# A two-layer hybrid decoder trunk on one core: five small reorderings on VectorE, ScalarE and TensorE

## The chip, the cores and the metric

The kernel runs on one core of one Trainium2 chip. The metric is the device time of one execution in microseconds (us), as a median over runs. The engines are called as the profile calls them: PE is TensorE (PEld its weight loads), DVE is VectorE, ACT is ScalarE, POOL is GpSimd, and SP issues most of the DMAs.

## The reference

The reference is a trunk of two layers on a sequence of 512 tokens of width 1024. Each layer is this, cut to what matters here:

```
h = rms_norm(x, norm1_g);  proj = h @ w_in
y_a = gelu(a_u) * (tril(w_spatial) @ rms_norm(gelu(a_v)) + b_spatial)      # mixer A: gMLP
y_b = causal attention, 8 heads, on low-rank q and kv, rotary tail          # mixer B
y_c = gated DeltaNet, 8 heads, chunks of 64, on silu(causal_conv(c_qkv))    # mixer C
      (q and k of each head l2-normalised; a triangular solve in each chunk; a scan over 8 chunks)
y_c = rms_norm(y_c) * silu(c_z)
x = x + (sum_i sigmoid(gate_i) * (y_i @ w_branch[i])) @ w_out
x = x + relu(rms_norm(x) @ w_ff1)^2 @ w_ff2
```

All of it is fp32. The kernel gets near-fp32 matmuls by splitting each large operand into a high and a low part of fp32r and adding three passes (high by high, high by low, low by high).

## The kernel before

The whole stream is held transposed, channels on partitions and the 512 tokens along the free side. All weights come as one stream of 288 units of 512 KB. SP issues their DMAs into a ring of two raw slots, POOL splits each into high and low (lines 408 and 413, one operation each over 128x1024), and PE uses them in a fixed order, `UNITS`. Each engine has its own written-out program, and semaphores with running counts tie them together, so an instruction that waits holds everything behind it on its engine.

PE's unit of work is `project(tile)`: 24 matmuls of 128x512 (lines 445 to 447) into one of two alternating PSUM banks. A later tile of the same bank waits for `bank_read`, which DVE or ACT raise when they have taken the last one out. Small matmuls and transposes of the mixers are set between the projections.

In each layer PE projects the decay row, then twelve tiles k0 to k3, q0 to q3, v0 to v3 (i = 0 to 11). For tile i DVE runs `conv(i)` (lines 1559 to 1566) and ACT `take_conv(i)`: Silu, and for the eight tiles of k and q a Square into the buffer `csq`. PE then sums the squares by head in `sum_squares(i)` (line 535, matmuls with two output columns). `csq` has four slots of 2 KB. In layer 0 DVE also works out the angles of the rotary tables in `rotation_angles(0)` and `(1)`, on tiny tiles.

Then comes the triangular solve. DVE runs 31 rank-one steps (lines 1672 and 1675) and large transposes (1691, 1696), and in between takes tiles that PE has ready: `token_rows(tt)` (lines 1642, 1644, which raise `tok_scaled`) and `take_lat(j)`. PE waits for `tok_scaled` before it transposes `krT` (line 819), and for the last of DVE's transposes before `corner_products` (line 652). ACT places the products of the corner with four copies (line 1232), in two pairs. After that a recurrence of nine steps begins, `recur(step)`: PE, ACT's copy of `vnew` (line 1258), PE again (line 710), DVE's `state`. ACT takes the four z tiles with Silu in `take_z(j)`, and loads the table for Sqrt ahead of the corner copies (line 1227).

While the delta branch is merged, DVE masks the spatial weights with the lower triangle (line 1776, 128x1024, raises `wsp_masked`) between two of its steps. Attention follows: 32 blocks of scores, each with ACT's Exp (line 1348), and for each group of eight blocks `take_sums(i)` (line 1326) and `outputs_high(i)` (1330) on ACT, and `normalise(i)` and `outputs_low(i)` (1886, 1891) on DVE. After the last Exp ACT loads the table for Gelu, runs four Gelus over `avT`, then takes the last sums, squares two tiles of `avT`, runs `outputs_high(3)`, and squares the last two. PE, after a projection of gates, sums those squares in `sum_av` (line 958), then waits for `wsp_masked` and transposes the masked weights (line 961).

ACT holds one table of functions at a time. A table load stands in the profile as ACT_TABLE_LOAD, at the line of the function that needs it, or at the line of an explicit `preload_act_table`. Copy and Square need none of their own.

Of the kernel before, what the change touches and what calls it, by code (L numbers as in the profile page):

```python
# [16 lines left out]
P = 128  # L17
DEPTH = 2
SEQ = 512
# [164 lines left out]
def hybrid_trunk(nc, stream, params, x, positions, constants, out):  # L184

    with ExitStack() as ctx:
# [46 lines left out]
        kqT, vT = at(0, "kqT", [P, 2, PAIRS, SEQ]), at(16, "vT", [P, PAIRS, SEQ])  # L233
        convd, csq = at(84, "convd", tile2), at(56, "csq", [P, 4, SEQ])
        gtok, gone = at(68, "gtok", [P, TT, STACK]), at(69, "gone", [P, 2, TT, HEADS])
# [198 lines left out]
        def _(pe):  # L434
            pe.wait_ge(ident_in, 16)
            for layer in range(DEPTH):
# [93 lines left out]
                def sum_squares(i):  # L530

                    pe.wait_ge(csq_ready, layer * per.csq_ready + i + 1)
                    for t in range(TT):
                        at = (i // 4 * TT + t) * HEADS + 2 * (i % 4)
                        last = mm(S(0)[:, at:at + 2], csq[:, i % 4, t * P:(t + 1) * P], c("ind", i % 4, 8)[:, 2 * (i % 4):2 * (i % 4) + 2],  # L535
                                  start=True, stop=True)
                    last.then_inc(csq_summed, 1)
# [254 lines left out]
                for i in range(12):  # L792
                    if i or layer:
                        project((("k", "q", "v")[i // 4], i % 4))
                    for n in {3: (0,), 4: (1,), 5: (2,), 6: (3,), 7: (4, 5), 8: (6, 7)}.get(i, ()):
                        sum_squares(n)
                    if i == 5:
                        turn_decay()
                    if i == 7:
                        cumulate()  # L800
                    if i == 9:
                        turn_rows()
                        pe.wait_ge(consts_done, 1)
                    if i >= 10:
                        for tt in range(2):
                            chunk_terms(2 * (i - 10) + tt)
# [234 lines left out]
        def _(act):  # L1041
# [50 lines left out]
            for layer in range(DEPTH):  # L1092
# [31 lines left out]
                def take_conv(i):  # L1124
# [5 lines left out]
                    if i < 8:  # L1130
                        act.wait_ge(act_tile, layer * per.act_tile + i + 1)
                        if i >= 4:
                            act.wait_ge(csq_summed, layer * per.csq_summed + i - 3)
                        f(csq[:, i % 4], dst, ACT.Square).then_inc(csq_ready, 1)

# [82 lines left out]
                for hf in range(2):  # L1218
# [5 lines left out]
                    if hf == 0:  # L1224
                        take_z(2)
                take_z(3)
                nc.scalar.preload_act_table(ACT.Sqrt)
                for hf in range(2):
                    for ch in range(2):
                        rows = np.s_[64 * ch:64 * ch + 32]  # L1230
                        act.wait_ge(corner_done, layer * per.corner_done + 2 * hf + ch + 1)
                        nc.scalar.copy(gated[rows, 2 * hf:2 * hf + 2, 0, :, 32:64],
                                       S((4 + 2 * hf + ch) % 6)[rows].rearrange("p (t h s) -> p t h s", t=2, h=HEADS)).then_inc(corner_placed, 1)

                def square_o(tt):
# [9 lines left out]
                def copy_output(step):  # L1245
# [6 lines left out]
                    if step and step % 2 == 0:  # L1252
                        square_o(step // 2 - 1)

                for step in range(CHUNKS + 1):
                    rows = np.s_[0:64] if step == 0 else np.s_[64:128] if step == CHUNKS else np.s_[0:128]
# [80 lines left out]
                for n in range(32):  # L1337
# [14 lines left out]
                    if n % 8 == 6 and n > 8:  # L1352
                        outputs_high(n // 8 - 1)
                nc.scalar.preload_act_table(ACT.Gelu)
                for j in range(4):
                    tile = TILE_NO[("av", j)]
                    act.wait_ge(bank_read[tile % 2], layer * per.bank_read + tile // 2 + 1)
                    f(avT[:, j], avT[:, j], ACT.Gelu).then_inc(av_ready, 1)
                take_sums(3)
                act.wait_ge(av_ready, layer * per.av_ready + 4)  # L1360
# [53 lines left out]
        def _(dve):  # L1414
# [83 lines left out]
            nc.vector.tensor_scalar(tri[:], c("incl"), -1.0, None, ALU.is_ge).then_inc(tri_done, 1)  # L1498
            rotation_angles(0)
            for layer in range(DEPTH):  # L1500
# [90 lines left out]
                for i in range(9):  # L1591
# [9 lines left out]
                    if i == 5:  # L1601
# [6 lines left out]
                        ins.then_inc(g_token, 1)  # L1608
                    if i == 5 and layer == 0:
                        rotation_angles(1)  # L1610
                dve.wait_ge(cum_done, layer * per.cum_done + 1)
# [58 lines left out]
                for k in range(31):  # L1670
# [9 lines left out]
                    if k == 11:  # L1680
                        token_rows(2)
                        take_lat(3)
                    if k == 15:
                        token_rows(3)
                    if k == 17:
                        take_lat(4)
# [76 lines left out]
                def latent(d):  # L1763
# [7 lines left out]
                    if 1 <= d < 6:  # L1771
                        dve.wait_ge(lat_hi, layer * per.lat_hi + d)
                        tt_(latLo[:, d - 1], ltmp[:, (d - 1) % 2], latHi[:, d - 1].bitcast(F32), ALU.subtract).then_inc(lat_lo, 1)
                    if d == 6:
                        dve.wait_ge(tables_in, 64)
                        tt_(p("wsp").rearrange("p (g n) -> p g n", g=8), p("wsp").rearrange("p (g n) -> p g n", g=8),
                            c("tril").unsqueeze(1).broadcast_to([P, 8, P]), ALU.mult).then_inc(wsp_masked, 1)

# [128 lines left out]
                normalise(3)  # L1907
                outputs_low(3)
                nc.vector.memset(biasr[:].bitcast(F32), 0.0).then_inc(vector_step, 1)
                dve.wait_ge(vector_step, steps.next())  # L1910
# [180 lines left out]
```

## Time and profile before

| | |
|---|---|
| median of 3 runs | 1855.63 us (1855.09 to 1856.7) |
| the profiled execution, its own time | 1855.63 us |
| its span, first to last instruction | 1853.8 us |
| mean granted PE clock | 0.998 of full |
| PE busy | 1832.8 us, 99% of the span |
| DVE, ACT, POOL busy | 869.0, 467.0, 1032.4 us |
| weights read | 288 units of 512 KB |

The span is the time between the profile's first and last instruction. The profiled execution's own time is 1.8 us more than its span, and it is also the median of the runs shown. Times in rows are counted from the start of the span. Matmuls are pipelined and their ends are modelled, so the distance between two starts tells more of PE than a duration does. Layer 0 runs to about 925 us and layer 1 repeats it 915.5 us later.

### The profile page before, as it was taken

Reading aid. Unit: us, or ns where it says so; the run is one execution under the profiler, and the core shown is the slowest. Engines: PE = TensorE matmul, PEld = TensorE weight load, DVE = VectorE, ACT = ScalarE, POOL = GpSimd, SP = SyncE. Lnnn points to the kernel's source line nnn. Section 1 sums busy time; section 2 is a strip of 40 time slices with the busy share of each in tenths; the row PEclk is TensorE's granted clock in tenths of the full one; section 3 lists DMA queues with packets and bytes.
Section 4 is the critical chain, followed back from the end, with each engine's and each line's share of the span. In section 5 each row is a group of like instructions: output and inputs, shape, how many; then the busy total and the mean of one; then the engine's idle time right before and its main releaser. Section 6 shows DMA issues by size and latency. Waiting matters only on the chain.

```text
span 1853.8 us, 26960 instructions
## 1 busy us (share of the span) xinstructions
PE 1832.8 (99%) x10428; PEld 1491.7 (80%) x10428; DVE 869.0 (47%) x1283; ACT 467.0 (25%) x872; POOL 1032.4 (56%) x580
## 2 busy tenths in 40 slices
PE   8999999999999999999999999999999999999998
PEld 7887788778888888888888777886788888888887
DVE  8587546543444322323265965465444442414141
ACT  6433315550113000000144242165411230001010
POOL 6534267225666666666653524661456666666662
PEclk9999999999999999999999999999999999999999
DMA  6212033122223333333342211221322233323331
GB/s 229 84 58 80 26 101 104 34 91 91 89 93 107 101 93 100 94 99 96 97 137 69 69 59 54 95 91 35 103 91 91 91 95 98 98 96 98 95 101 70
DMA packets 46762, 167.12 MB, mean 90 GB/s; under 512 B 5018, under 2 KB 8346, under 8 KB 46146
## 3 DMA queue, kind: packets, MB, share of 16 engines
q1 hardware_dynamic: 44066, 154.30, 26.7%
q10 hardware_dynamic: 2592, 11.29, 1.6%
q8 instruction: 83, 1.36, 0.3%
q14 instruction: 21, 0.17, 0.0%
HBM read 159.28 MB, written 6.29 MB: 89 GB/s over the span
## 4 chain that ended last, share of the span: by engine, by line
PE 88%; DVE 9%; issue 1%; ACT 1%; DMA 0%; POOL 0%; SPq 0%; ACTq 0%; DVEq 0%; POOLq 0%
PE ps L445 26%; PE ps L447 25%; PE ps L446 25%; PE ps L897 2%; DVE ps L1675 1%; DVE outer L1672 1%; PE ps L920 1%; DVE lanes L1659 1%; PE ps L907 1%; DVE gated L1696 1%; PE ps L535 1%; DVE acc L1446 1%; PE ps L678 1%; PE ps L710 1%; PE ps L688 1%
## 5 line engine op out<-in xcount | busy, mean ns | idle before, releaser
L413 POOL TENSOR_TENSOR wLo<-wraw,wHi 128x1024 fp32r<-128x1024 f32 x288 | 724.7, 2516 | 23.9
L408 POOL TENSOR_SCALAR wHi<-wraw 128x1024 fp32r<-128x1024 f32 x288 | 307.8, 1069 | 769.5 <-PE ps L447 754.0
L445 PE MATMUL ps<-hHi,wHi 128*128 128x512 f32 x1360 | 545.1, 401 | 1.7 <-DVE gated L1696 1.3
L447 PE MATMUL ps<-hHi,wLo 128*128 128x512 f32 x1360 | 530.9, 390 | 0.0
L446 PE MATMUL ps<-hLo,wHi 128*128 128x512 f32 x1360 | 530.3, 390 | 0.0
L445 PEld LDWEIGHTS ps<-hHi,wHi 128*128 128x128 f32 x1360 | 256.0, 188 | 66.1 <-issue 11.1
L447 PEld LDWEIGHTS ps<-hHi,wLo 128*128 128x128 f32 x1360 | 255.6, 188 | 54.4
L446 PEld LDWEIGHTS ps<-hLo,wHi 128*128 128x128 f32 x1360 | 256.2, 188 | 49.7 <-issue 1.2
L445 PE MATMUL ps<-fHi,wHi 128*128 128x512 f32 x640 | 249.3, 389 | 0.0
L447 PE MATMUL ps<-fHi,wLo 128*128 128x512 f32 x640 | 249.0, 389 | 0.0
L446 PE MATMUL ps<-fLo,wHi 128*128 128x512 f32 x640 | 249.0, 389 | 0.0
L1396 ACT ACTIVATE fHi<-relu 128x512 fp32r<-128x512 f32 x64 | 40.6, 634 | 555.3 <-DVE relu L1952 555.3
L1966 DVE TENSOR_TENSOR xT<-xT,ps 128x512 f32<-128x512 f32 x56 | 38.5, 687 | 254.8 <-PE ps L447 254.8
L446 PEld LDWEIGHTS ps<-fLo,wHi 128*128 128x128 f32 x640 | 120.1, 188 | 25.0
L447 PEld LDWEIGHTS ps<-fHi,wLo 128*128 128x128 f32 x640 | 120.1, 188 | 25.0
L445 PEld LDWEIGHTS ps<-fHi,wHi 128*128 128x128 f32 x640 | 120.1, 188 | 24.7
L1952 DVE SCALAR_TENSOR_TENSOR relu<-ps,rstdT 128x512 f32<-128x512 f32 x64 | 44.2, 691 | 193.8 <-PE ps L447 185.9
L1509 DVE TENSOR_TENSOR ps<-ps,rstdT 128x512 f32<-128x512 f32 x56 | 39.0, 696 | 97.1 <-PE ps L447 96.9
L1112 ACT ACTIVATE sg<-ps 128x512 f32<-128x512 f32 x48 | 28.5, 598 | 184.2 <-DVE ps L1509 184.2
L447 PE MATMUL ps<-bHi,wLo 128*128 128x512 f32 x192 | 74.7, 389 | 0.0
L445 PE MATMUL ps<-bHi,wHi 128*128 128x512 f32 x192 | 74.7, 389 | 0.0
L446 PE MATMUL ps<-bLo,wHi 128*128 128x512 f32 x192 | 74.7, 389 | 0.0
(299 smaller groups left out, 2022.4 us busy)
## 6 DMA issues: line engine op xcount, KB each, us to landing
wraw<-stream SPq DMA_DIRECT2D x288, 512.0 KB, 3.5
out<-xT ACTq DMA_DIRECT2D x2, 2048.0 KB, 9.4
xT<-out ACTq DMA_DIRECT2D x2, 2048.0 KB, 7.9
xin<-x SPq DMA_DIRECT2D x4, 512.0 KB, 6.2
out<-ost ACTq DMA_DIRECT2D x1, 1024.0 KB, 4.1
out<-ost ACTq DMA_DIRECT2D x2, 512.0 KB, 3.8
prm<-params ACTq DMA_DIRECT2D x1, 647.0 KB, 4.1
prm<-params SPq DMA_DIRECT2D x1, 576.0 KB
```

Of the source, the lines that this page charges most:

```text
L408: nc.gpsimd.tensor_scalar(wHi[:, slot], wraw[:, slot % RAW], 1.0, 0.0, ALU.mult, ALU.add).then_inc(unit_high, 1)
L413: nc.gpsimd.tensor_tensor(wLo[:, slot], wraw[:, slot % RAW], wHi[:, slot].bitcast(F32), ALU.subtract).then_inc(unit_split, 1)
L445: mm(o, lh[lc], rh[rc], start=start, stop=False)
L446: mm(o, lh[lc], rl[rc], start=False, stop=False)
L447: return mm(o, ll[lc], rh[rc], start=False, stop=stop)
L535: last = mm(S(0)[:, at:at + 2], csq[:, i % 4, t * P:(t + 1) * P], c("ind", i % 4, 8)[:, 2 * (i % 4):2 * (i % 4) + 2], start=True, stop=True)
L897: mm(bank[:, 0:w], qhT[0:QK, h, i * P:w], khT[0:QK, h, 0:w], start=True, stop=False)
L1112: f(gate[:, d % 2], bank_of(TILE_NO[tile]), ACT.Sigmoid).then_inc(bank_read[TILE_NO[tile] % 2], 1)
L1396: f(fHi[q % 2][:, n], relu[:, n % 2], ACT.Square).then_inc(f_hi, 1)
L1509: return tt_(o, bank_of(TILE_NO[tile]), rstdT[:], ALU.mult)
L1952: stt(relu[:, n % 2], bank_of(n), 0.0, rstdT[:], ALU.max, ALU.mult).then_inc(relu_done, 1)
L1966: tt_(xT[:, d], xT[:, d], sums_bank(d), ALU.add).then_inc(x_added, 1)
```

## The change

Seven edits, of which several belong together.

- PE and ACT, `csq`: the buffer goes from four slots to two. The sum for tile i-2 now follows projection i, for i from 2 to 8, and that of tile 7 follows projection 8 as well. ACT's Square of tile i waits until the sum of tile i-2 is done. The order before was tiles 0 to 3 one at a time after projections 3 to 6, tiles 4 and 5 together after 7, and 6 and 7 together after 8.
- DVE, layer 0: `rotation_angles(0)` moves from ahead of the layer to behind `conv(1)`.
- DVE: `token_rows(3)` moves from behind solve step 15 to behind step 17, ahead of `take_lat(4)`.
- ACT: `take_z(3)` moves from ahead of the four corner copies to between the first and the second.
- ACT: the preload of the Sqrt table moves from ahead of the corner copies to behind the fourth, directly ahead of the recurrence.
- ACT: the preload of the Gelu table is removed, and `take_sums(3)` moves ahead of the four Gelus.
- DVE: the mask of the spatial weights moves from the merge of the delta branch to behind `outputs_low(3)`.

```diff
-        convd, csq = at(84, "convd", tile2), at(56, "csq", [P, 4, SEQ])
+        convd, csq = at(84, "convd", tile2), at(56, "csq", tile2)
...
-                        last = mm(S(0)[:, at:at + 2], csq[:, i % 4, t * P:(t + 1) * P], c("ind", i % 4, 8)[...],
+                        last = mm(S(0)[:, at:at + 2], csq[:, i % 2, t * P:(t + 1) * P], c("ind", i % 4, 8)[...],
...
                 for i in range(12):
                     if i or layer:
                         project((("k", "q", "v")[i // 4], i % 4))
-                    for n in {3: (0,), 4: (1,), 5: (2,), 6: (3,), 7: (4, 5), 8: (6, 7)}.get(i, ()):
-                        sum_squares(n)
+                    if 2 <= i < 9:
+                        sum_squares(i - 2)
                     if i == 5:
                         turn_decay()
                     if i == 7:
                         cumulate()
+                    if i == 8:
+                        sum_squares(7)
...
-                        if i >= 4:
-                            act.wait_ge(csq_summed, layer * per.csq_summed + i - 3)
-                        f(csq[:, i % 4], dst, ACT.Square).then_inc(csq_ready, 1)
+                        if i >= 2:
+                            act.wait_ge(csq_summed, layer * per.csq_summed + i - 1)
+                        f(csq[:, i % 2], dst, ACT.Square).then_inc(csq_ready, 1)
...
-                take_z(3)
-                nc.scalar.preload_act_table(ACT.Sqrt)
                 for hf in range(2):
                     for ch in range(2):
                         rows = np.s_[64 * ch:64 * ch + 32]
                         act.wait_ge(corner_done, layer * per.corner_done + 2 * hf + ch + 1)
                         nc.scalar.copy(gated[...], S((4 + 2 * hf + ch) % 6)[...]).then_inc(corner_placed, 1)
+                        if hf == 0 and ch == 0:
+                            take_z(3)
...
+                nc.scalar.preload_act_table(ACT.Sqrt)
                 for step in range(CHUNKS + 1):
                     rows = np.s_[0:64] if step == 0 else np.s_[64:128] if step == CHUNKS else np.s_[0:128]
                     act.wait_ge(tr_done, layer * per.tr_done + step + 1)
...
-                nc.scalar.preload_act_table(ACT.Gelu)
+                take_sums(3)
                 for j in range(4):
                     tile = TILE_NO[("av", j)]
                     act.wait_ge(bank_read[tile % 2], layer * per.bank_read + tile // 2 + 1)
                     f(avT[:, j], avT[:, j], ACT.Gelu).then_inc(av_ready, 1)
-                take_sums(3)
...
-            rotation_angles(0)
             for layer in range(DEPTH):
...
-                    if i == 5 and layer == 0:
-                        rotation_angles(1)
+                    if i in (1, 5) and layer == 0:
+                        rotation_angles(i // 5)
...
-                    if k == 15:
+                    if k == 17:
                         token_rows(3)
-                    if k == 17:
                         take_lat(4)
...
-                    if d == 6:
-                        dve.wait_ge(tables_in, 64)
-                        tt_(p("wsp")..., p("wsp")..., c("tril")..., ALU.mult).then_inc(wsp_masked, 1)
...
                 outputs_low(3)
+                dve.wait_ge(tables_in, 64)
+                tt_(p("wsp")..., p("wsp")..., c("tril")..., ALU.mult).then_inc(wsp_masked, 1)
+
                 nc.vector.memset(biasr[:].bitcast(F32), 0.0).then_inc(vector_step, 1)
```

## Rows read from the trace of the kernel before

**Rows 1.** The page, busy time by engine: us, share, instructions.

```profile
PE 1832.8 (99%) x10428; PEld 1491.7 (80%) x10428; DVE 869.0 (47%) x1283; ACT 467.0 (25%) x872; POOL 1032.4 (56%) x580
```

**Rows 2.** Windows view around 70 us; PEclk is the granted clock.

```profile
69.05:72.47 3.42, 3.42 (x10) 2.65 (x9) 0.93 (x2) 2.37 (x3) 0.89 (x1) 0.50 0.38 96
```

**Rows 3.** Timeline of PE, narrow sums and the next projection, both layers.

```profile
65.98 1.84 PE L535 MATMUL ps<-cst,csq 128*128 128x2 f32 x16
...
68.46 0.50 PE L445 MATMUL ps<-hHi,wHi 128*128 128x512 f32 x1
...
75.40 0.39 PE L447 MATMUL ps<-hHi,wLo 128*128 128x512 f32 x1
...
985.52 0.50 PE L445 MATMUL ps<-hHi,wHi 128*128 128x512 f32 x1
...
990.86 0.39 PE L447 MATMUL ps<-hHi,wLo 128*128 128x512 f32 x1
```

**Rows 4.** Timeline of ACT around the start of the recurrence, layer 0.

```profile
172.43 1.28 ACT L1227 ACT_TABLE_LOAD   x1
175.21 1.18 ACT L1232 COPY gated<-ps 32x512 f32<-32x512 f32 x2 [1.50 <-PE ps L660]
...
180.48 0.36 ACT L1258 COPY vnew<-ps 64x256 f32<-64x256 f32 x1
```

**Rows 5.** Timeline of PE, the matmuls behind that copy.

```profile
180.90 0.67 PE L710 MATMUL ps<-vnew,kend 64*64 64x64 f32 x8 [0.17 <-ACT vnew L1258]
```

**Rows 6.** Timeline of ACT behind the last Exp, layer 0.

```profile
390.98 2.19 ACT L1358 ACTIVATE avT<-avT 128x512 f32<-128x512 f32 x4
394.05 0.59 ACT L1326 COPY spread<-ps 128x512 f32<-128x512 f32 x1 [0.88 <-PE ps L930]
394.53 1.16 ACT L1335 ACTIVATE asq<-avT 128x512 f32<-128x512 f32 x2
395.58 0.61 ACT L1330 CAST bHi<-ob 128x512 fp32r<-128x512 f32 x1
```

**Rows 7.** Timeline of PE, the transposes of the masked weights.

```profile
401.72 1.04 PE L961 MATMUL ps<-cst,prm 128*128 128x128 f32 x8
```

**Rows 8.** Timeline of POOL, three stretches of layer 0.

```profile
254.27 2.72 POOL L413 TENSOR_TENSOR wLo<-wraw,wHi 128x1024 fp32r<-128x1024 f32 x1
...
285.78 1.05 POOL L408 TENSOR_SCALAR wHi<-wraw 128x1024 fp32r<-128x1024 f32 x1 [1.99 <-PE ps L447]
...
399.74 2.35 POOL L413 TENSOR_TENSOR wLo<-wraw,wHi 128x1024 fp32r<-128x1024 f32 x1
```

**Rows 9.** Timeline of DVE beside the first two of those.

```profile
254.64 2.89 DVE L1773 TENSOR_TENSOR latLo<-ltmp,latHi 128x512 fp32r<-128x512 f32 x1
...
286.19 1.70 DVE L1776 TENSOR_TENSOR prm<-prm,cst 128x1024 f32<-128x1024 f32 x1
```

**Rows 10.** Timeline of PE, the fifth block of the kv projection.

```profile
290.53 0.39 PE L447 MATMUL ps<-wHi,latLo 128*128 128x512 f32 x1
290.89 0.47 PE L445 MATMUL ps<-wHi,latHi 128*128 128x512 f32 x1
```

**Rows 11.** Timeline of DVE, `take_lat(4)` behind solve step 17, layer 0.

```profile
146.54 0.69 DVE L1509 TENSOR_TENSOR latT<-ps,rstdT 128x512 f32<-128x512 f32 x1
```

**Rows 12.** Timeline of PE, the transposes of `krT` and the corner products.

```profile
146.02 0.43 PE L819 MATMUL ps<-cst,krT 32*128 32x32 f32 x4
...
171.02 0.50 PE L445 MATMUL ps<-hHi,wHi 128*128 128x512 f32 x1 [0.64 <-DVE gated L1696]
```

**Rows 13.** Timeline of DVE, first and last of `rotation_angles(0)`, and `conv(4)`.

```profile
20.77 1.03 DVE L1474 CAST posf<-posi 128x4 f32<-128x4 int32 x1
...
25.42 0.19 DVE L1491 TENSOR_SCALAR trig<-gy 128x64 f32<-128x64 f32 x1
...
49.20 2.31 DVE L1566 SCALAR_TENSOR_TENSOR convd<-ps,prm,convd 128x511 f32<-128x511 f32 x3
```

**Rows 14.** Timeline of PE, the first matmul of projection 6, layer 0.

```profile
54.03 0.50 PE L445 MATMUL ps<-hHi,wHi 128*128 128x512 f32 x1
```

More of the change, by code:

```diff
@@ L534, in sum_squares @@
                         at = (i // 4 * TT + t) * HEADS + 2 * (i % 4)
-                        last = mm(S(0)[:, at:at + 2], csq[:, i % 4, t * P:(t + 1) * P], c("ind", i % 4, 8)[:, 2 * (i % 4):2 * (i % 4) + 2],
+                        last = mm(S(0)[:, at:at + 2], csq[:, i % 2, t * P:(t + 1) * P], c("ind", i % 4, 8)[:, 2 * (i % 4):2 * (i % 4) + 2],
                                   start=True, stop=True)
@@ L1773, in latent @@
                         tt_(latLo[:, d - 1], ltmp[:, (d - 1) % 2], latHi[:, d - 1].bitcast(F32), ALU.subtract).then_inc(lat_lo, 1)
-                    if d == 6:
-                        dve.wait_ge(tables_in, 64)
-                        tt_(p("wsp").rearrange("p (g n) -> p g n", g=8), p("wsp").rearrange("p (g n) -> p g n", g=8),
-                            c("tril").unsqueeze(1).broadcast_to([P, 8, P]), ALU.mult).then_inc(wsp_masked, 1)
                 branch_merge(2, 0, latent)
@@ L1908, in _ @@
                 outputs_low(3)
+                dve.wait_ge(tables_in, 64)
+                tt_(p("wsp").rearrange("p (g n) -> p g n", g=8), p("wsp").rearrange("p (g n) -> p g n", g=8),
+                                       c("tril").unsqueeze(1).broadcast_to([P, 8, P]), ALU.mult).then_inc(wsp_masked, 1)
                 nc.vector.memset(biasr[:].bitcast(F32), 0.0).then_inc(vector_step, 1)
```

## The prediction

> **What bounds the kernel now.** The page comes first. PE is busy 99% of the span [rows 1], and no other engine comes near it. So an edit can lengthen the run only where PE comes to wait, and shorten it only where PE waits now or its clock is down. The second view is the granted clock by stretches. It stands at 1.00 from 11 us on, except in 69.05 to 72.47, where it is 0.50, that is 1.2 in place of 2.4 GHz [rows 2]. The third is the timeline of each engine at the seven edited places. There the question is which of PE's waits ends last, and how early the work that PE waits for is ready. One more thing is to be kept in mind: PE's sequence is fixed, so a delay of PE is passed on to the end unless PE already stood still for another engine further on. I found one such place, the wait for DVE's transposes at 171.02 [rows 12].
>
> The sum is made against the profiled execution's own time, 1855.63 us, which is also the median of the runs shown. Its span is 1.8 us less.
>
> **The Sqrt load, +1.29 us a layer.** Now the table is loaded at 172.43, and the first corner copy waits for PE until 175.21 with 1.50 us of idle time before it, so the load of 1.28 us is hidden [rows 4]. In the change it stands between the fourth corner copy and the copy of `vnew`. That copy now starts at 180.48, right behind the corner copies [rows 4]. It would start 1.28 + 0.01 us later, at 181.77. PE's state update at 180.90 waits for exactly this copy already [rows 5]; between the two PE has only one eighth of a projection, which it does now as well. Behind PE's update stand DVE's `state`, then the next step, and so the whole recurrence; nothing there waits for anything that does not hang on PE. The two layers give 2.58 us. `take_z(3)`, now between the first and the second corner copy, takes 0.6 us there; the second copy would end near 176.9, and PE begins the recurrence only at about 179.2, so it costs nothing.
>
> A rule of the Trainium skill speaks of a higher price: "ScalarE: Activation LUTs", section "What ACT_TABLE_LOAD costs", gives 1.28 us for the load and 1.38 us more for a drain, 2.66 us at every switch. The rows show the first part only, since the corner copies after 172.43 and the Gelus at 390.98 stand without such a gap. By the rule this term would be 2 x 2.66 = 5.3 us, not 2.6.
>
> **The late Gelus and the late mask, +2.03 us a layer.** These two edits meet in one place, and I follow one layer.
>
> - Now ACT does the Gelu load and the four Gelus, 2.19 us, before it waits for PE's spread sums, and `take_sums(3)` comes at 394.05 with 0.88 us of idle time before it [rows 6]. So they are hidden. In the change `take_sums(3)` keeps its time, since PE sets it, and ends at 394.64. Then come the load (1.28) until 395.94, the four Gelus (2.19) until 398.14, and the first two squares (1.16) until 399.33.
> - The cast of `outputs_high(3)` now starts 1.05 us behind the start of the two squares and takes 0.61 [rows 6]. In the change it ends at 398.17 + 1.05 + 0.61 = 399.83, against 396.19 now.
> - PE wants the squares from about 398.2 on, and has finished with them by 401.72, where the transposes of the masked weights begin [rows 7]. With the first square ready at about 398.8 and each later one tied to PE's own progress, `sum_av` would end about 0.6 us later, at 402.3. This alone would cost 0.6.
> - DVE's `outputs_low(3)` waits for that cast, and would ask to start at 399.86. It reads two operands from SBUF. POOL's operation of 2.35 us starts at 399.74 [rows 8]; PE's progress sets that, not ACT. How the two get on is seen in another place: DVE's operation of the same kind at 254.64 took 2.89 us, until 257.53, while POOL's ran from 254.27 to 256.99 [rows 8, 9]. It ended 0.54 us behind POOL's. So `outputs_low(3)` would end 0.54 behind 402.09, at 402.63.
> - Then comes the mask. It took 1.70 us at 286.19, with POOL's operation running until 286.83 [rows 8, 9]; it ended at 287.89, 1.06 behind POOL's. I take 1.06, since POOL has nothing to do just then. The mask ends at 403.69. PE starts about 0.06 behind a release, as it does at 171.02 behind DVE. That gives 403.75 in place of 401.72, 2.03 us later, and 4.06 over two layers.
>
> Bounds of the term: 0.6 a layer from the squares alone, and 2.7 with the mask at its full 1.70. Behind it nothing more is late: DVE now stands idle for 7 us until ACT's `ainv`, and this time shrinks with PE's delay.
>
> At its old place the mask is gone. It stood ahead of DVE's last merge step, on which ACT's copies of the kv projection wait. PE lost a little there: from 290.53 to 290.89 it is 0.36 between two starts, against 0.23 in a steady run, 0.13 too much [rows 10]. I take this as given back, -0.26 over both layers.
>
> **Two slots of `csq`, regrouped sums: 0.** The number of matmuls is the same, and only their grouping changes. The sum behind projection i needs the square of tile i-2, whose DVE and ACT work has the whole of projections i-1 and i, twice 5.34 us, and even the late `conv(4)` of layer 0 is done at 51.51 [rows 3, 13]. ACT's new wait is for a sum that stands directly behind the projection of its own tile, while DVE still needs 2.31 us and more for that tile's convolution [rows 13]. Behind that Square on ACT is only the next tile. If the regrouping costs or gives anything, it is a tenth of a us a layer.
>
> **The clock, -1.60 us.** At 65.98 PE does two narrow sums and the cumulating matmuls, 2.48 us until 68.46 in which it writes only 2 to 32 columns at a time [rows 3]. Right behind it the granted clock falls [rows 2]. The projection from 68.46 to the start of its last matmul takes 6.94 us, and the same one in layer 1 takes 5.34, from 985.52 to 990.86 [rows 3]. So the fall cost 1.60 us. In the change one of the two sums stands a projection earlier, and the narrow piece is near 1.6 us. The next piece now, behind projection 8, is 1.7 us long with no fall, so I take it that none comes. Against it: layer 1 has the same 2.48 us and no fall, so the length alone does not decide. Bounds: -1.60, or 0.
>
> **`rotation_angles(0)`: 0.** It now takes from 20.77 to 25.61 [rows 13], while PE is busy with what is there. Behind `conv(1)` it delays `conv(2)` to `conv(4)`. The last of these ends at 51.51, and PE needs that bank at 54.03 for projection 6 [rows 13, 14], a cover of 2.5 us. With all 4.84 us it would be late by 2.3. Two of its operations, at 20.77 and behind, took a microsecond and more beside POOL, where they otherwise take 0.2, and the first convs start earlier by what is cleared away. So I take 0, with 2.3 as the bound above.
>
> **`token_rows(3)` two steps later: 0.** It would end where `take_lat(4)` starts now, 146.6 [rows 11], and PE waits for it at 146.02 [rows 12]. PE is held up by 0.64. But at 171.02 PE now stands still for 0.64 until DVE's transposes are there, and DVE's work up to then is the same in sum [rows 12]. So the delay is taken out of that wait. The bound above is 0.64 a layer.
>
> **Sum.** 2.58 + 4.06 - 0.26 - 1.60 = +4.78 us, so 1855.63 + 4.78 = 1860.4 us, 0.26% slower.
>
> **Rivals.**
>
> - The mask does not hold PE, 12 in 100. `outputs_low(3)` misses POOL's operation by 0.12 us only. If the cast ends before 399.7, DVE goes first, and if the mask gets in behind it, it is done before PE asks at 402.3. Against it: POOL then waits and would be next. A layer would cost 0.6 in place of 2.03, in all 1860.4 - 2.9 = 1857.5 us. This is the case of the other side, no slower than can be told.
> - The Sqrt load is hidden, 8 in 100, if ACT can load while it waits for the fourth corner product. Against it: it stands behind the copy in order. 1857.8 us.
> - The clock falls all the same, or falls at one of the new waits of PE, 14 in 100: 1862.0 us.
> - The rotation or the late token rows come onto PE's path, 5 in 100: up to 2.3 more, 1862.7 us.
> - Each table switch has a hidden drain, 3 in 100. It would show as time between a load and its neighbours, of which the rows have none. For 1.4 us more at each of the two Sqrt loads it gives 1863.2 us (the mask would still set the other place); the rule quoted above says this.
>
> **How the numbers follow.** The forecast itself has 56 in 100, and 2 are left for a gain that I don't see. A measurement of this kernel can tell 0.2%, 3.7 us, from no change, so slower means above 1859.3. The forecast lies only 1.1 us above that, and I count 47 of its 56 as slower, 9 as the same. With 14 + 5 + 3 slower is 0.69; the same is 9 + 12 + 8 = 0.29; faster 0.02. The range from 1857.3 to 1862.6 takes in the two cheap cases and the case of the clock, and leaves out some of the last two.
>
> **What would show it.** In the profile after: ACT's load between the last corner copy and `vnew`, and PE's state update with an idle time of about 1.5 us before it; PE's transposes of the mask with about 1.4 us of waiting for DVE; `outputs_low(3)` near 2.8 us long; a clock of 1.00 behind 68 us; no wait of PE at 171. The prediction is wrong if PE gets to the mask with no wait, or if the clock falls in a place that I don't name.

## The result, and the profile after

| | before | after |
|---|---|---|
| median | 1855.36 us (1855.09 to 1856.7, 4 runs) | 1870.44 us (1866.58 to 1871.3, 4 runs) |
| the profiled execution, its own time | 1855.63 us | 1870.5 us |
| its span | 1853.8 us | 1868.7 us |
| mean granted PE clock | 0.998 | 0.994 |

The change makes the kernel 15 us slower: the medians lie 15.1 us apart, 0.81%, and the ratio over all the runs is 1.0076, with a 95% interval of 1.0058 to 1.0093. The forecast was 5 us, and 1870.4 lies far outside its range. One execution of after took 1866.58 us, with a mean granted clock of 0.998, and the others 1869.79 to 1871.3 with 0.994 or 0.995. So not every execution has the falls of the clock that the profile below shows, or not as long.

First the page of after, busy time by engine. It is nearly that of before [rows 1]: PE has the same 10428 instructions and is busy 6.6 us longer. The other 8.3 us of the longer span are idle.

```profile
PE 1839.4 (98%) x10428; PEld 1496.6 (80%) x10428; DVE 874.4 (47%) x1283; ACT 467.7 (25%) x872; POOL 1030.7 (55%) x580
```

Next the waits of PE in after: what PE waited for, us in total, times, the longest.

```profile
PE ps L459 <- DMA xin<-x: 5.1, 1, 5.1
PE ps L710 <- ACT vnew L1261: 4.0, 8, 1.5
PE ps L535 <- ACT csq L1136: 2.9, 1, 2.9
PE ps L963 <- DVE prm L1906: 2.3, 2, 1.1
PE ps L678 <- DVE state L1749: 1.6, 7, 0.2
PE ps L960 <- ACT asq L1338: 1.1, 2, 0.5
PE ps L821 <- DVE rhsv L1645: 1.1, 2, 0.5
```

Before, the same view has the first at 5.0 us, `vnew` at 1.8 with 0.2 as the longest, `state` at 1.8, and 1.3 us for DVE's transposes in `gated`; `csq`, `prm`, `asq` and `rhsv` are not there. Four of the new waits were forecast (`vnew`, `prm`, `asq`, `rhsv`, of which the last takes the place of the one for `gated`). The 2.9 us for `csq` were not.

Then the windows of after. The columns are the stretch, its us, the busy us and instructions of PE, PEld, DVE, ACT and POOL, the granted clock, the DMA share and GB/s. 

```profile
49.06:55.88 6.82, 6.04 (x18) 5.17 (x19) 6.64 (x8) 1.09 (x3) 2.37 (x1) 0.50 0.36 133
69.05:72.47 3.42, 3.42 (x18) 2.83 (x17) 0.98 (x2) 1.26 (x2) 0.84 (x1) 1.00 0.36 132
185.59:192.42 6.83, 6.38 (x59) 5.35 (x61) 1.27 (x3) 1.12 (x4) 0.13 (x1) 0.50 0.22 79
1107.19:1114.02 6.83, 6.83 (x81) 5.79 (x81) 1.38 (x4) 0.74 (x2) 0.00 (x0) 0.50 0.22 79
```

The fall of before at 69.05 [rows 2] is gone. Three new ones have come, each twice as long. The first begins while PE stands still for `csq`, the second while it stands still for `vnew` at the start of the recurrence, and the third 0.2 us behind the same wait in layer 1.

The 14.9 us of span can be followed on PE's fixed sequence. I took each matmul of after less the same matmul of before, and read where this difference changes:

| where | forecast | measured, layer 0 | layer 1 |
|---|---|---|---|
| start: clock up sooner, weights, other small steps | 0 | -0.5, +0.1 | +0.1 |
| wait of the third sum for `csq` | 0 | +2.9 | - |
| clock fall from 49.06 | 0 | +3.1 | - |
| clock fall of before at 69.05, gone | -1.60 | -1.59 | - |
| token rows, 0.6 late and absorbed at DVE's transposes | 0 | -0.1 | 0 |
| Sqrt load ahead of the recurrence | +1.29 a layer | +1.28 | +1.31 |
| clock fall in the recurrence | 0 | +2.2 | +2.3 |
| merge without the mask | -0.13 a layer | -0.22 | -0.20 |
| squares late (0.8, 0.8) and mask late (1.4, 1.4) | +2.03 a layer | +2.15 | +2.17 |

The terms that the forecast had priced come to +4.8 in its sum and, by the rows of the table that belong to them, to 2.59 + 4.32 - 0.42 - 1.59 = +4.90 as measured. What it missed is 6.0 us around the third sum and 4.5 us of clock in the two recurrences. The small steps are -0.3 and -0.1. All of it makes 15.0, and PE's last matmul is 14.9 late; the rest is rounding.

The place at the start, in the timelines of after (start, us, engine, operation, idle time before and its releaser). DVE:

```profile
36.30 0.77 DVE L1476 CAST posf<-posi 128x4 f32<-128x4 int32 x1
...
37.36 2.28 DVE L1483 TENSOR_SCALAR gy<-gy 128x64 f32<-128x64 f32 x1
39.68 0.19 DVE L1485 TENSOR_SCALAR gy<-gy 128x64 f32<-128x64 f32 x1
39.91 3.69 DVE L1488 SCALAR_TENSOR_TENSOR gy<-gy 128x64 f32<-128x64 f32 x3
43.64 0.95 DVE L1493 TENSOR_SCALAR trig<-gy 128x64 f32<-128x64 f32 x1
44.63 0.70 DVE L1560 TENSOR_TENSOR ps<-ps,rstdT 128x512 f32<-128x512 f32 x1
```

POOL beside it:

```profile
37.13 2.46 POOL L413 TENSOR_TENSOR wLo<-wraw,wHi 128x1024 fp32r<-128x1024 f32 x1
...
41.12 2.40 POOL L413 TENSOR_TENSOR wLo<-wraw,wHi 128x1024 fp32r<-128x1024 f32 x1
```

ACT and PE behind it:

```profile
48.50 0.63 ACT L1131 ACTIVATE kqT<-convd 128x512 f32<-128x512 f32 x1 [9.05 <-DVE convd L1567]
49.16 0.63 ACT L1136 ACTIVATE csq<-kqT 128x512 f32<-128x512 f32 x1
...
49.84 1.87 PE L535 MATMUL ps<-cst,csq 128*128 128x2 f32 x8 [2.88 <-ACT csq L1136]
```

`rotation_angles(0)` takes from 36.30 to 44.59, 8.29 us, where it took 4.84 at its old place [rows 13]. Each of its operations on 64 elements a partition takes some 0.2 us when POOL lets it, and otherwise until POOL's current operation has ended: the one at 37.36 ends at 39.64, POOL's from 37.13 at 39.59. Therefore `conv(2)` starts only at 44.63, ACT's square for it is ready at 49.79, and PE's third sum starts at 49.84. By the Trainium skill, "SBUF — State Buffer", section "SBUF: two separate sides", GpSimd and those VectorE operations that run in a two-port mode, or read two inputs from SBUF, hold a shared pair of ports exclusively, and the one that comes second waits out the other's whole instruction. The trace agrees, with 0.05 us between the two ends; in which mode these operations ran it does not show.

The same two places in before, `conv(2)` on DVE and ACT's square for it:

```profile
36.32 0.69 DVE L1559 TENSOR_TENSOR ps<-ps,rstdT 128x512 f32<-128x512 f32 x1
...
41.42 0.63 ACT L1134 ACTIVATE csq<-kqT 128x512 f32<-128x512 f32 x1
```

So `conv(2)` is 8.3 us late, the whole length of the rotation, and its square 7.7.

The start of the recurrence in after, ACT and then PE:

```profile
183.13 1.18 ACT L1232 COPY gated<-ps 32x512 f32<-32x512 f32 x2 [2.31 <-PE ps L660]
184.32 1.28 ACT L1257 ACT_TABLE_LOAD   x1
185.62 0.36 ACT L1261 COPY vnew<-ps 64x256 f32<-64x256 f32 x1
...
186.04 1.11 PE L710 MATMUL ps<-vnew,kend 64*64 64x64 f32 x8 [1.46 <-ACT vnew L1261]
```

This is the chain of the forecast: the load comes between the last corner copy and `vnew` [rows 4], and the wait of PE goes from 0.17 [rows 5] to 1.46. The eight matmuls behind it take 1.11 us, since the clock is at half its level by then.

The end of attention in after, ACT, DVE and PE:

```profile
401.15 0.59 ACT L1329 COPY spread<-ps 128x512 f32<-128x512 f32 x1 [4.38 <-PE ps L932]
401.76 1.28 ACT L1361 ACT_TABLE_LOAD   x1
403.05 2.19 ACT L1361 ACTIVATE avT<-avT 128x512 f32<-128x512 f32 x4
405.27 1.15 ACT L1338 ACTIVATE asq<-avT 128x512 f32<-128x512 f32 x2
406.33 0.60 ACT L1333 CAST bHi<-ob 128x512 fp32r<-128x512 f32 x1
...
406.96 2.77 DVE L1887 TENSOR_TENSOR bLo<-ob,bHi 128x512 fp32r<-128x512 f32 x1 [4.50 <-ACT bHi L1333]
409.66 1.21 DVE L1906 TENSOR_TENSOR prm<-prm,cst 128x1024 f32<-128x1024 f32 x1
...
410.93 1.09 PE L963 MATMUL ps<-cst,prm 128*128 128x128 f32 x8 [1.14 <-DVE prm L1906]
```

Against before [rows 6, 7] all stands as forecast: the load, the four Gelus and the squares one behind the other, then the cast, and DVE's `outputs_low(3)` at 2.77 us beside POOL's operation from 406.84 to 409.19. The mask took 1.21 where I had 1.06, and PE's wait for it is 1.14 where I had about 1.4, since the squares had already made PE 0.8 late and not 0.6.

### The profile page after: what moved, and what is told of

It reads as the page before. It is cut to its first block, busy times and chain, and to the rows that moved or that the text cites. A ratio compares the mean times of both kernels' runs of the same rounds, so it can differ in the third digit from the quotient of the medians.

```text
span 1868.7 us, 26963 instructions
## 1 busy us (share of the span) xinstructions
PE 1839.4 (98%) x10428; PEld 1496.6 (80%) x10428; DVE 874.4 (47%) x1283; ACT 467.7 (25%) x872; POOL 1030.7 (55%) x580
## 4 chain that ended last, share of the span: by engine, by line
PE 88%; DVE 8%; ACT 2%; issue 1%; DMA 0%; SPq 0%; ACTq 0%; DVEq 0%
PE ps L445 25%; PE ps L447 25%; PE ps L446 25%; PE ps L899 2%; PE ps L922 1%; DVE lanes L1660 1%; PE ps L909 1%; DVE ps L1676 1%; DVE outer L1673 1%; PE ps L535 1%; PE ps L710 1%; PE ps L678 1%; DVE convd L1567 1%; DVE acc L1448 1%; PE ps L688 1%
```

## The experiments

The first group of runs undoes one part of the change each. The second does one part alone on the kernel before. Unless said otherwise, the rest of the kernel is unchanged. The kernel before ran beside them and had a median of 1855.52 (14 runs, 1853.59 to 1857.36), 1853.86 (14, 1853.46 to 1857.0) and 1855.1 us (26, 1853.38 to 1857.34) on the three chips. Its own runs spread by some 4 us, which sets how finely medians can be told apart. The ratios are over all the runs and differ from those of the medians by up to 0.001 (b_sqrt_only: 1.0043 by the medians, 1.0033 as given). The kernel after was not run again beside these runs, so a difference to its median compares two measurements. Where it matters I also give PE's distance: the start of a matmul in a run's profile less the start of the same matmul in the profile of before.

### The rotation back ahead of the layer (a_rot_back, on the kernel after)

```diff
+            rotation_angles(0)
             for layer in range(DEPTH):
...
-                    if i in (1, 5) and layer == 0:
-                        rotation_angles(i // 5)
+                    if i == 5 and layer == 0:
+                        rotation_angles(1)
```

> The kernel after, with rotation_angles(0) back ahead of layer 0, all else as changed. Theory (the rotation is the cause in layer 0: it took 8.3 us behind conv(1), beside POOL's operations, so that PE waited 2.9 us for the square of tile 2 and its clock then fell for 6.8 us): PE's wait at the third sum and the fall of the clock at 49 us both go, 6.0 us in all, to about 1864.5 us. Rival (the two slots and the earlier sums are the cause): the wait stays at least in part, and the time stays within 2 us of 1870.4.

Measured: 1865.66 us (1864.24 to 1866.57, 4 runs), 4.8 less than after; the span of the profile is 1862.5, 6.2 less. The wait for `csq` is gone: from projection 4 to projection 6 PE's distance to before doesn't grow, where it grows by 6.0 us in after. The clock fall in this stretch is gone as well, in the windows of a_rot_back:

```profile
49.06:55.88 6.82, 6.82 (x38) 5.77 (x37) 4.23 (x7) 1.53 (x3) 3.79 (x3) 1.00 0.45 148
```

The falls in the recurrences remain (from 182.62 and 1104.22); the second lasts 3.4 us here and 6.8 in after and is 1.1 us cheaper, while PE is 0.6 us later at the first two sums here. The 6 us at the start are the rotation's, a wait and a fall of the clock together.

### Is it the early sums, or the rotation? (a_sums_back, b_rot_only, b_sums_only)

The first puts `csq` and the order of sums of before back into the kernel after. The second moves the rotation alone in the kernel before. The third does the two slots and the regrouped sums alone.

```diff
-                    if 2 <= i < 9:
-                        sum_squares(i - 2)
+                    for n in {3: (0,), 4: (1,), 5: (2,), 6: (3,), 7: (4, 5), 8: (6, 7)}.get(i, ()):
+                        sum_squares(n)
```

> The kernel after, with four slots of csq and the sums in their old places; the rotation stays behind conv(1). Theory (the rotation alone): DVE ends conv(4) near 59.2 us as in the kernel after, and PE, which no longer waits at the third sum, waits for the bank of projection 6 from 54 us on, about 5 us, so the time does not fall, and stays at 1869 to 1873 us. Rival (it takes both edits, since a sum that comes one projection later has its cover): no wait in layer 0, about 1864.5 us, with the fall of the clock behind the cumulating matmuls possible again (1.6 us more).

> The kernel before with one edit, rotation_angles(0) behind conv(1). Theory: rotation_angles(0) takes about 8 us there, PE waits about 5 us for the bank of projection 6, and the clock may fall behind that wait (3 us more): 1860 to 1864 us. Rival (it takes both edits): 1855 us, as before.

> The kernel before with one edit, two slots of csq and the sums spread to one behind each projection. Theory: no wait of PE in either layer, and no fall of the clock behind the cumulating matmuls, where the kernel before has one of 3.4 us: 1853.8 us, 1.6 us faster, or as before if the kernel before has the fall in only part of its executions. Rival (the sums by themselves make PE wait): 1858 us or more.

Measured: a_sums_back 1873.49 us (1872.3 to 1873.82, 4 runs), 3 more than after and just above what was expected. b_rot_only 1863.42 (1860.87 to 1864.13, 5 runs), ratio 1.004 [1.0026, 1.0054]. b_sums_only 1854.2 (1853.98 to 1855.72, 10 runs), ratio 0.9991 [0.9982, 1.0001].

With the sums late the wait doesn't go. PE runs on for one more projection and then stands still longer at the bank for projection 6, as the timeline of a_sums_back shows:

```profile
59.38 0.79 PE L445 MATMUL ps<-hHi,wHi 128*128 128x512 f32 x1 [5.63 <-DVE convd L1565]
```

In b_rot_only the wait is at the same place, and up to 5.9 us long, and the rotation takes 10.62 us. Here DVE's timeline of b_rot_only, the last operation of the rotation:

```profile
44.64 2.40 DVE L1491 TENSOR_SCALAR trig<-gy 128x64 f32<-128x64 f32 x1
```

One operation of 0.2 us takes 2.40 here and 0.95 in after. So the rotation alone makes the wait, and its place in the order among POOL's operations sets how long it is. The early sums made nothing worse, they only met the delay sooner. Alone they are free, and the profile of b_sums_only shows a clock of 1.00 behind its start. (That execution took 1855.72, the highest of the ten; the clock came up only at 13.52 us in it, at 11.03 in the profile of before, and PE was 1.4 us later from there on. The other nine took 1853.98 to 1854.41.)

### The rotation with one operand in PSUM (a_rot_psum, on the kernel after)

If it is POOL that holds the rotation up, its scratch in a free bank of PSUM should help without moving it.

```diff
-                cyc = gy[:, 0, TT * 16:2 * TT * 16].rearrange("p (t r) -> p t r", t=TT)
+                room = ps[:, 4] if n == 0 else gy[:, 0]
+                cyc = room[:, TT * 16:2 * TT * 16].rearrange("p (t r) -> p t r", t=TT)
```

> The kernel after, with one of the two scratch tiles of rotation_angles(0) in a free PSUM bank. Theory (DVE's small operations with both sides in SBUF wait out whole operations of POOL: 8 small operations took 8.3 to 10.6 us in place of about 1.9): five of the eight now have one side in PSUM and take 0.2 us each, rotation_angles(0) takes 2 to 5.3 us in the same place, PE does not wait at the third sum, the clock does not fall there, and the time is that of the kernel with the rotation back, 1865.7 us. Rival (the wait is the price of DVE's work at that place, whatever POOL does): it stays above 8 us, and the time at 1870.4 us.

Measured: 1864.54 us (1864.53 to 1864.79, 4 runs), 5.9 less than after. DVE and POOL in its timelines:

```profile
37.70 0.23 DVE L1486 TENSOR_SCALAR ps<-ps 128x64 f32<-128x64 f32 x1
37.96 0.74 DVE L1489 SCALAR_TENSOR_TENSOR gy<-ps,gy 128x64 f32<-128x64 f32 x3
38.74 0.98 DVE L1494 TENSOR_SCALAR trig<-gy 128x64 f32<-128x64 f32 x1
...
37.20 2.47 POOL L413 TENSOR_TENSOR wLo<-wraw,wHi 128x1024 fp32r<-128x1024 f32 x1
```

Five operations from 37.44 on now run at 0.23 to 0.25 us each while POOL's stands from 37.20 to 39.67. Only the last, which reads and writes SBUF, waits it out: it ends at 39.72. The rotation takes 3.45 us in place of 8.29, PE doesn't wait for `csq`, its distance doesn't grow there, and the clock doesn't fall there. This shows the mechanism in the same place with the same order.

### The Sqrt load alone, and with PE kept busy (b_sqrt_only, b_sqrt_fill, on the kernel before)

```diff
-                nc.scalar.preload_act_table(ACT.Sqrt)
                 for hf in range(2):
...
+                nc.scalar.preload_act_table(ACT.Sqrt)
                 for step in range(CHUNKS + 1):
```

The second kernel adds work to this, six matmuls of 128x512 into a bank that nobody reads, where PE waits for `vnew`:

```diff
+                    if step == 0:
+                        for n in range(FILL):
+                            mm(S(4), hHi[:, 0, 0:P], hHi[:, 1], start=True, stop=True)
                     pe.wait_ge(vnew_done, layer * per.vnew_done + step + 1)
```

> The kernel before with one edit, the preload of the Sqrt table behind the four corner copies. Theory: the copy of vnew starts 1.28 us later and PE stands still for about 1.5 us there; then the clock falls to half for 6.8 us in the recurrence, which costs about 2.2 us more: 3.4 to 3.6 us a layer, 1862.3 us. Rival (the clock fell for another reason, such as the layout of the whole): only 1.28 us a layer, 1858.0 us.

> The same, with six extra matmuls of 128x512 (1.36 us of work, into a free PSUM bank that nobody reads) that PE does while it waits for vnew at step 0. They are extra work, and leave the output alone. Theory (the clock falls because PE stands still there): PE is not idle, the clock stays at 1.00 and the time is that of the load alone, 1858.0 us. Rival (the clock falls because of the narrow matmuls of the recurrence, or by chance): the fall stays, 1862.3 us or a little more.

Measured: b_sqrt_only 1861.85 us (1859.45 to 1862.44, 5 runs), ratio 1.0033 [1.0019, 1.0047]. b_sqrt_fill 1858.55 us (1856.02 to 1859.98, 10 runs), ratio 1.002 [1.001, 1.003]. By the medians the kernel with more work is 3.3 us faster, though the two ranges overlap by 0.5 us. PE and the window of b_sqrt_only:

```profile
180.02 0.67 PE L710 MATMUL ps<-vnew,kend 64*64 64x64 f32 x8 [1.46 <-ACT vnew L1258]
...
182.68:189.51 6.83, 6.80 (x92) 5.47 (x93) 1.87 (x5) 1.10 (x3) 0.00 (x0) 0.50 0.02 7
```

And of b_sqrt_fill:

```profile
180.47 1.53 PE L707 MATMUL ps<-hHi 128*128 128x512 f32 x6
182.09 0.68 PE L714 MATMUL ps<-vnew,kend 64*64 64x64 f32 x8
...
182.68:189.51 6.83, 6.25 (x118) 4.81 (x118) 2.95 (x7) 1.47 (x4) 0.00 (x0) 1.00 0.25 79
```

In b_sqrt_only the fall begins 2.7 us behind the start of PE's update. With the filling ACT still copies `vnew` right behind its load, and PE's update starts as late behind the load as without; all of it stands 2 us later since this profile has the clock fall behind the cumulating matmuls, at 68.86, and the other has not. But the clock stays at 1.00 in the stretch where it was 0.50, and in the recurrence of layer 1 too. PE's distance grows by 3.55 and 3.63 us over the start of the two recurrences in b_sqrt_only, and by 1.30 and 1.27 in b_sqrt_fill. So the falls come from the wait and not from the 64x64 matmuls of the recurrence alone, which are the same in all kernels; before has no fall there. The filling does two things at once, it ends the standing still and adds dense work, and no run parts the two. The load costs 1.28 + 1.31, and the falls that it brings 4.5 in the profile of after and 4.6 in that of b_sqrt_only: more than the load.

### The end of attention (a_mask_back, a_gelu_back, b_gelu_mask)

a_mask_back puts the mask back at the merge. a_gelu_back puts the preload of the Gelu table back and `take_sums(3)` behind the Gelus. Both are on the kernel after. b_gelu_mask does both edits alone in the kernel before.

```diff
-                take_sums(3)
+                nc.scalar.preload_act_table(ACT.Gelu)
                 for j in range(4):
...
+                take_sums(3)
```

> The kernel after, with the mask of the spatial weights back at the merge of the delta branch; the late Gelus stay. Theory: of the 2.0 us a layer at sum_av only the late squares remain, 0.6 to 0.7; 1.4 us a layer are given back and 0.15 a layer lost at the kv projection: 1870.4 - 2.5 = 1867.9 us. Rival (the late Gelus alone cost all of it): 1870.4 us.

> The kernel after, with the Gelu preload back and take_sums(3) behind the Gelus; the mask stays late. Theory: outputs_low(3) starts near 396.2 us as before, ahead of POOL's operation, and the mask is done about 2 us before PE asks for it, so the whole 2.0 us a layer goes: 1866.3 us. Rival (the mask alone is late): PE still waits for it, 1868 us or more.

> The kernel before with two edits, the late Gelus and the late mask. Theory: PE begins the transposes of the masked weights 2.0 to 2.1 us later in each layer and gains 0.15 us at the kv projection: 3.8 us slower than the kernel before on the same chip. Rival (the two together also let the clock fall there): 5 us or more slower.

Measured: a_mask_back 1870.15 us (1865.1 to 1871.96, 4 runs), a_gelu_back 1867.43 (1863.37 to 1867.65, 4 runs), b_gelu_mask 1859.38 (1857.66 to 1860.84, 9 runs), ratio 1.0025 [1.0016, 1.0035].

The median of a_mask_back misses its expectation, 0.3 us less than after in place of 2.5. The profile says why in part: the rotation, which this edit doesn't touch, took 10.57 us in it, the wait for `csq` 5.2, and with its fall this place cost 7.6 us, 1.7 more than in after. The falls of the recurrences were 3.41 and 10.24 us long, which together cost 0.3 more than the two of 6.83. The waits of PE in a_mask_back:

```profile
PE ps L535 <- ACT csq L1136: 5.2, 1, 5.2
...
PE ps L960 <- ACT asq L1338: 1.1, 2, 0.5
```

At the place of the edit it did what was expected: the wait for `prm` is gone, and PE's distance to before grows by the 0.8 us of the late squares in each layer, where it grew by 2.2 in after. In a_gelu_back the waits for `prm` and for `asq` are both gone, though the mask stays late, and PE's distance doesn't grow there. Its median is 1.1 above what was expected: its wait for `csq` was 4.8 us, and that place cost 8.0 with its fall, 2.1 more than in after, against 1.2 less for a shorter fall in layer 1. So the late mask alone is hidden, and it costs 1.4 a layer only behind the late Gelus, which delay the cast ahead of it. b_gelu_mask shows both without the rotation, in its waits (`asq` has 1.1 us in two here too):

```profile
PE ps L961 <- DVE prm L1905: 2.3, 2, 1.2
```

PE's distance to before grows by 2.2 us in each layer, and the clock doesn't fall at these waits.

### Three edits back, and a kernel from the rest (a_three_back, b_best)

a_three_back is the kernel after with the rotation and the Gelu edit as they were before, and with the Sqrt preload ahead of the recurrence again, now behind `take_z(3)`, between the first two corner copies. It keeps two slots of `csq`, the regrouped sums, the late token rows, `take_z(3)` between the corner copies and the mask behind `outputs_low(3)`. b_best is the kernel before with the two slots and regrouped sums, and the mask in attention:

```diff
+                    if n == 21:
+                        tt_(p("wsp")..., p("wsp")..., c("tril")..., ALU.mult).then_inc(wsp_masked, 1)
```

> The kernel after, with the rotation, the Sqrt preload (now behind take_z(3), between the first and second corner copy) and the Gelu edit back. What is left of the change: two slots of csq with spread sums, take_z(3) between the copies, token_rows(3) two steps later, the mask behind outputs_low(3). Theory: these four cost nothing, and the time is that of the spread sums alone, 1854.2 us. Rival (one of them costs by itself, the late mask or the late token rows): 1855.5 us or more.

> The kernel before with two slots of csq and the spread sums, and the mask of the weights in the middle of attention (behind block 21, where DVE is idle half of the time). Theory: no fall of the clock behind the cumulating matmuls, and 0.26 us less at the kv projection: 1853.9 us, 0.1% faster than the kernel before in the median and with less spread. Rival (the mask delays a block of attention by POOL's operations): 1855 us or more.

Measured: a_three_back 1853.81 us (1853.52 to 1854.08, 10 runs), ratio 0.9995 [0.9986, 1.0004]. b_best 1853.71 us (1853.51 to 1854.02, 11 runs), ratio 0.9996 [0.9987, 1.0005]. Windows of b_best:

```profile
13.50:925.00 911.50, 906.72 (x5173) 738.39 (x5172) 433.23 (x644) 232.04 (x438) 520.75 (x291) 1.00 0.29 91
925.00:1852.10 927.10, 916.42 (x5224) 745.66 (x5222) 423.30 (x622) 227.50 (x422) 504.99 (x283) 1.00 0.27 87
```

All that the change costs lies in three of its edits. The rest costs nothing, the wait for `rhsv` included, which a_three_back still has at 1.1 us; in its profile PE is 0.6 us late at the first two sums, and in that of b_best it is not. Both kernels have a median 1.3 to 1.4 us below that of before, and their runs lie within 0.6 us where those of before lie 4 apart. That is what the clock fall behind the cumulating matmuls would explain. Of the profiles of the six kernels with two sums ahead of those matmuls (before, a_sums_back, b_rot_only, b_sqrt_only, b_sqrt_fill, b_gelu_mask), each has a fall of 3.41 us there in one layer or in both, seven in twelve places. The eight kernels with the regrouped sums have none in sixteen. And the runs of before lie in three groups, 1853.4 to 1854.1, 1855.0 to 1855.9 and 1856.7 to 1857.4, as none, one and two falls of 1.6 us would make them. The interval doesn't separate either from 1, so a gain is not shown.

## Why the prediction was wrong

The direction was right, the size was not.

- **The Sqrt load** was right: 1.28 and 1.31 us for 1.29. The drain of 1.38 us of "ScalarE: Activation LUTs", section "What ACT_TABLE_LOAD costs", in the Trainium skill, is not seen: the load ends at 185.60 and `vnew` is copied from 185.62. The corner copies of before, which I named against a drain, say nothing of it, since they stand 1.50 us behind their load [rows 4]; after shows it better.
- **The late Gelus and the late mask** were right: 2.15 and 2.17 for 2.03. The rival in which the mask slips in behind the cast didn't come about.
- **The merge, the token rows, `take_z(3)` and the regrouped sums** were right, the merge with -0.22 and -0.20 for -0.13 a layer. **The old fall of the clock** went, and gave back the 1.6 us forecast.
- **"`rotation_angles(0)`: 0" failed, in two ways.** The first is its duration. I took the 4.84 us of its old place as an upper bound, and said that beside POOL its operations take a microsecond and more, but counted this only as a reason for less. It took 8.29 to 10.6 us at the new place. Nor did the cleared start of the layer give anything: `conv(0)` was 1.4 us earlier, but `conv(1)` scaled its tile from 33.28 against 33.30. The second is the cover. I took the 2.5 us ahead of projection 6, but the regrouped sums ask for tile 2 earlier, behind projection 4. I had examined the sums with the rotation still out of the way. There, in before, the square was ready at 42.05; PE asks at 46.96 in after, so the cover was 4.9, and a square 7.7 us later makes 2.8 of waiting, as measured. At projection 6 the old cover gives 8.3 - 2.5 = 5.8 us of waiting, and a_sums_back shows 5.6.
- **The clock failed as a rival.** "The clock falls all the same, or falls at one of the new waits of PE" had 14 in 100 and 1.6 us. I had priced it as one fall, of the size of the old one. In each of the seven profiles with the long wait for `vnew` (1.46 us) the clock fell in it or within 2.7 us behind the start of PE's update, in both layers, for 6.83 us in nine of the fourteen cases, which costs 2.2 in after. It need not do so in every execution: the shortest of after, 1866.58 us, had a mean clock of 0.998 against 0.994 in the profiled one, and the shortest of b_sqrt_only, 1859.45, 0.997 against 0.995. The fall at the wait for `csq` cost 3.1. A new wait of PE of this size should have been priced as a wait plus a fall, in the main sum.
- **The range** reached only to one rival at a time, with the rotation's bound at 2.3. The two that came together are 6.0 + 4.5 = 10.5 us.

What stays open: why the mask's wait of 1.14 us brings no fall, in after and in b_gelu_mask, when that of 1.46 ahead of `vnew` does. They differ in length and in what PE does around them, and no run tells these apart. Nor was it tried why the narrow block behind projection 7 brings a fall in some places and not in others, or why a fall is at times 3.41 and at times 6.83 us long at the same place. The rotation took about 8.3 us in two profiles (after, a_sums_back) and 10.6 in three (b_rot_only, a_mask_back, a_gelu_back), and its starts differ by a tenth of a us only, so how much of this changes from execution to execution is not known.

## What to carry to other kernels

Small operations on VectorE must not be costed by their own length where GpSimd works without a pause: count each as one that may wait for the end of GpSimd's current operation, or give it an operand in PSUM. On a kernel in which TensorE is always busy, a new wait of a microsecond and a half costs itself and can bring a stretch at half clock that is dearer than the wait, as it did in every profile here that has one in the recurrence; look at the granted clock first, and fill a wait that can't be avoided. When several edits meet on one chain, recount each one's cover with all the others made.

## What the runs showed of the hardware

- Eight DVE operations of 64 elements a partition took 1.9 us in all in `rotation_angles(1)` of before, with POOL idle beside them. The eight of `rotation_angles(0)`, seven of that size and a cast of 4 elements, took 4.84, 8.29 and 10.6 beside POOL's operations, and 3.45 with an operand of five of them in PSUM.
- Falls of the granted clock to 0.50, that is from 2.4 to 1.2 GHz, lasted 3.41 or 6.83 us (once 10.24, in a_mask_back at 1108.18), and cost 1.6 us (3.41 in projections), 3.1 (6.83 from PE's wait for `csq` on) and 2.2 (6.83 in the recurrence, where PE isn't the only bound). Of 3.41 us they cost 1.0 to 1.2 in the recurrence (a_rot_back, a_sums_back, a_mask_back, a_gelu_back).
- Behind a run of matmuls with 2 to 32 output columns of some 2.5 us the clock fell in seven of twelve places; with one sum taken out of it, in none of sixteen.
- Six useless matmuls in a wait of PE made the kernel 3.3 us faster by the medians than the same kernel without them, 1858.55 against 1861.85, and 4.6 us by PE's distance in the two profiles, with no fall in either recurrence.
